# GpSimd's four stores of a turned tile ahead of the next tile load, in a hybrid mLSTM / RWKV-7 / attention / PEER layer

## The reference, cut to what matters

```python
# per block of 128 tokens, 8 heads, 16 experts of 16384 a head
top, pos = lax.top_k(cand, PK_TOPK)          # cand: sums of two sets of 16 scores
eidx = jnp.take_along_axis(cidx, pos, axis=-1)
gate = jax.nn.softmax(top, axis=-1)
act = jax.nn.gelu(jnp.einsum('thkd,td->thk', u_tab[eidx], xb), approximate=False)
return jnp.einsum('thk,thkd->td', gate * act, v_tab[eidx])
```

## Time and profile before

| | |
|---|---|
| time, median of 3 runs | 2667.21 us (2660.73 to 2667.88) |
| the profiled execution | 2662.08 us, of which the span from first to last instruction is 2660.3 us |
| TensorE busy, matmuls | 2383.6 us, 90% of the span |
| VectorE busy | 1722.8 us, 65% |
| GpSimd busy | 693.2 us, 26% |
| mean granted TensorE clock | 0.939 of full speed |
| tile loads by GpSimd (L532) | 120, of which 106 at depth 2 |
| stores of turned tiles (L537) | 512 |

### The profile page before, as it was taken

How to read it: one execution, slowest core, us unless ns; L and a number is a source line. 1 busy time by engine, 2 the same in 40 slices (tenths; PEclk the granted TensorE clock), 3 DMA queues, 4 the chain that set the end, 5 groups by cost and what they waited for, 6 DMA issues and landing times.

```text
span 2660.3 us, 41336 instructions
## 1 busy us (share of the span) xinstructions
PE 2383.6 (90%) x16321; PEld 2195.8 (83%) x16321; DVE 1722.8 (65%) x3186; ACT 914.0 (34%) x1569; POOL 693.2 (26%) x1003
## 2 busy tenths in 40 slices
PE   7976796887668989989899987999999999999997
PEld 5954675875546978888799987999999999999996
DVE  3545376434642444448979987887786478878876
ACT  2222243210111111112234355777784333333332
POOL 3300000011430555425521200333333032332330
PEclk9987898996886999999999989999999999999999
DMA  4520320013752899757775746999999799999993
GB/s 145 185 57 11 113 56 17 20 43 104 242 182 99 281 289 302 242 171 252 231 239 192 240 154 187 319 336 317 323 323 360 266 326 348 343 348 343 350 346 116
DMA packets 323185, 586.48 MB, mean 220 GB/s; under 512 B 26704, under 2 KB 217184, under 8 KB 321456
## 3 DMA queue, kind: packets, MB, share of 16 engines
q1 hardware_dynamic: 222960, 274.07, 31.5%
q0 software_dynamic: 81600, 282.49, 30.9%
q10 hardware_dynamic: 18432, 27.27, 2.8%
HBM read 455.09 MB, written 128.64 MB: 219 GB/s over the span
## 4 chain that ended last, share of the span: by engine, by line
PE 44%; DVE 13%; DMA 10%; ACT 3%; POOL 2%; issue 2%; ACTq 0%; DVEq 0%; POOLq 0%
PE PS L1075 43%; DMA u_rows<-arena 3%; DVE LO L2146 2%; DMA RAW<-in_uT 2%; DMA u_rows<-CBLK 2%; DMA GU<-u_rows,EIDX 2%; DVE OH L2279 2%; POOL u_rows L537 2%; DVE GU L2288 2%; ACT OH L1017 1%; ACT HI L979 1%; DVE arena L2243 1%; DVE arena L1677 1%; DVE arena L2234 1%; DVE arena L1638 1%
## 5 line engine op out<-in xcount | busy, mean ns | idle before, releaser
L2146 DVE TENSOR_TENSOR LO<-RAW,HI 128x1024 fp32r<-128x1024 f32 x256 | 313.1, 1225 | 234.5 <-ACT HI L979 233.8
L979 ACT ACTIVATE HI<-RAW 128x1024 fp32r<-128x1024 f32 x256 | 270.3, 1056 | 551.5 <-PE PS L1075 503.7
L1075 PE MATMUL PS<-HT,W 128*128 128x272 f32 (+1 forms) x1536 | 374.9, 405 | 18.5 <-DVE HT L1689 12.5
L1075 PE MATMUL PS<-XH,HI 128*128 128x416 f32 x1024 | 369.8, 361 | 10.1 <-issue 8.4
L1075 PEld LDWEIGHTS PS<-HT,W 128*128 128x128 f32 (+1 forms) x1536 | 292.2, 192 | 94.8 <-issue 18.4
L1075 PE MATMUL PS<-XH,LO 128*128 128x416 f32 x1024 | 364.1, 356 | 0.0
L1075 PE MATMUL PS<-WH,HI 128*128 128x416 f32 x1024 | 360.4, 352 | 1.4 <-DVE WL L2161 1.4
L1075 PE MATMUL PS<-XL,HI 128*128 128x416 f32 x1024 | 361.6, 353 | 0.0
L1075 PE MATMUL PS<-WL,HI 128*128 128x416 f32 x1024 | 359.6, 351 | 0.0
L1075 PE MATMUL PS<-WH,LO 128*128 128x416 f32 x1024 | 357.4, 349 | 0.0
L1075 PE MATMUL PS<-arena 64*64 64x64 f32 (+10 forms) x3864 | 275.0, 261 | 49.8 <-DVE arena L1638 23.6
(11 more groups left out here) (262 smaller groups left out, 3639.8 us busy)
## 6 DMA issues: line engine op xcount, KB each, us to landing
RAW<-in_uT SPq DMA_DIRECT2D x128, 512.0 KB, 5.3
RAW<-in_vT SPq DMA_DIRECT2D x128, 512.0 KB, 5.7
arena<-in_uT POOLq DMA_DIRECT2D x90, 512.0 KB, 5.3
W<-in_w_in SPq DMA_DIRECT2D x58, 512.0 KB, 5.4
u_rows<-arena POOLq DMA_DIRECT2D x216, 128.0 KB, 4.0
table_a<-AX ACTq DMA_DIRECT2D x128, 208.0 KB, 4.6
gate_table<-GST SPq DMA_DIRECT2D x13, 2048.0 KB, 13.7
AIN<-table_a SPq DMA_DIRECT2D x128, 208.0 KB, 6.7
```

What stands on the lines that cost most here:

```text
L979: nc.scalar.activation(HI[:, s % NRING], RAW[:, s % NRING], ACT.Copy).then_inc(S("hi"), 1)
L1075: return nc.tensor.matmul(out, lhsT, rhs, start=first, stop=last)
L2146: dve.tensor_tensor(LO_[:, s % NRING], RAW[:, s % NRING], HI[:, s % NRING].bitcast(F32), ALU.subtract).then_inc(S("lo"), 1)
```

## The change

In the stages of depth 2, GpSimd issues the four stores of tile k first and the load of tile i = k + 2 behind them. In the stages of depth 1 the order stays: load, then stores. The load is moved into a function of its own, and nothing else differs: the same DMAs, buffers, semaphores and waits.

```diff
+            def load_tile(phase, i):
+
+                first, n, depth = TILES[phase]
+                if i < first + n and phase != "E":
+                    pool.dma_start(tile_in[phase][(i - first) % depth],
+                                   a["uT"][:, tile_chunk(i)].rearrange("p k n -> p (k n)")).then_inc(S(f"tin{i % 2}"), 16)
+
             def turn_tiles(phase):

                 first, n, depth = TILES[phase]
                 for i in range(first, first + n + depth):
                     k = i - depth
                     if k >= first:
                         pool.wait_ge(S("tr"), k + 1)
-                    if i < first + n and phase != "E":
-                        pool.dma_start(tile_in[phase][(i - first) % depth],
-                                       a["uT"][:, tile_chunk(i)].rearrange("p k n -> p (k n)")).then_inc(S(f"tin{i % 2}"), 16)
+                    if depth == 1:
+                        load_tile(phase, i)
                     if k >= first:
                         rows, turned = u_rows[tile_chunk(k)].rearrange("(b c) q x -> q c b x", b=4), tile_out[phase][(k - first) % depth]
                         for q in range(4):
                             pool.dma_start(rows[q], turned[32 * q:32 * q + 32].rearrange("c (b x) -> c b x", b=4)
                                            ).then_inc(S(f"tout{k % 2}"), 16)
+                    if depth == 2:
+                        load_tile(phase, i)
                 for i in range(2):
                     pool.wait_ge(S(f"tout{i}"), 64 * ((first + n + 1 - i) // 2))
```

## The result

The changed kernel takes 2679.06 us, median of 7 runs (2672.27 to 2681.64), against 2666.69 us for the kernel before (7 runs, 2660.73 to 2668.43). The ratio is 1.0056, with a 95% interval of 1.004 to 1.0072: slower. The two medians lie 12.4 us apart, the ratio stands for 15 us, and the interval holds both. The profiled execution took 2679.06 us, its span is 2677.3 us, 17.0 us over the span before. 2676 us was forecast.

A forecast was written before the change was run, and what follows sets the result against it. The loop of turning tiles was taken to bound stage G, and DVE's list the end of Q. G 6.6, A 0.9 and Q 2.1 us sum to 9.6 us on the 2667.2 us median, so 2676 us, range 2658 to 2690.

The forecast's parts named there:

- The bound: Stage G: the loop of turning tiles, 9.50 us, sets the pace, though TensorE is busy 191.3 of 206 us.
- The swap of the last DMA: Depth-2 loops: last issue stays at the same moment but becomes a 512 KB load instead of a 128 KB store.
- The signs: G: 30 or more of 44 waits on loads, landing 5.5 to 6.5 us, loop 9.8; first PEER product 10 us later.
- The three terms of the sum: Added time at 0.3 us a tile: G 22 loops, 6.6 us; A 3 loops, 0.9; Q 7 transposes, 2.1.
- X: Time in a tile's loop from GpSimd's first issue to the last landing, some 7.88 us in G; forecast to grow 0.3.
- X in a quiet queue: Last landing with little other traffic: 5.4 us before, 6.3 after, so growth of 0.9 us (0.84 unrounded).
- the estimate of one third of the way: Growth per loop taken one third from full queue (0) to quiet queue (0.9 us): 0.3 us.
- Q: End of stage Q: DVE's list sets TensorE's 8.40 us gap, so seven transposes each 0.3 us later cost 2.1 us.
- Order doesn't matter: Rival for G, A, Q: queue full enough, loop grows 0 to 0.2 us, 2667 to 2673 us; chance 0.32.
- The stores were the slow part, and the load lands soon enough: Rival: load lands within 5.1 us, loop falls up to 0.56 us, 2650 or 2658 us; chance of faster 0.13.
- The load is in the open everywhere: Rival: full 0.84 us per loop, G 18.5, A 2.5, Q 5.9, 27 us, so 2694 us; chance 0.13 (above 0.5).

The follow-up runs named there:

- g3_stores_first: Kernel before plus a third input buffer in stage G, with the four stores issued ahead of the load there: 2641.96 us, ratio 0.9928.
- g3_load_first: Kernel before plus a third input buffer in stage G, load still issued first: 2660.62 us, ratio 0.9994.
- the quarter loads: Two kernels, G's loads cut to 256 of 1024 columns against the kernel before: 2645.3 us load first, 2640.1 us stores first, one run each.
- the two experiments on the parts: Kernel before with stores ahead of the load in G alone: 2673.24 us, 1.0039; in N, A and Q alone: 2671.85 us, 1.003.
- gq3_stores_first: Kernel before plus a third input buffer and stores ahead of the load in both G and Q: 2642.63 us, ratio 0.9924.
- the run second: Kernel before with the load issued behind one store and ahead of three in every stage of depth 2: 2680.4 us, one run.

## Why the prediction was right

*The bound.* That the loop of transposes sets G, and not TensorE with its 93%, is shown by g3_stores_first against g3_load_first: the same DMAs and buffers in another order, a shorter loop, and 19 us less.

*The swap of the last DMA.* The step "the last DMA of a loop is issued at the same moment as before; it is now a load of 512 KB in place of a store of 128 KB" is shown by the chain after, by the 41 waits that moved from stores to loads, and by the quarter loads, which take the difference in size away and the loss with it.

*The signs.* Named beforehand were waits on the load, 30 or more (41), its landing at 5.5 to 6.5 us (6.0), a loop of 9.8 us (9.87), and TensorE's wait at about 20 us (22.7). The first PEER product was to start 10 us later; it started 17.0 us later.

*The size.* The three terms of the sum were all too small:

| place | forecast | the profiled pair | means of all profiles of either order |
|---|---|---|---|
| one loop in G | +0.3 us | +0.37 us | +0.30 us by one parity, +0.38 by all 44 transposes |
| G | +6.6 us | +10.1 | +8.1 |
| A | +0.9 us | +3.2 | +3.4 |
| Q | +2.1 us | +3.8 | +5.0 |
| all | +9.6 us | +17.0 | +12.4 by the medians |

The last column's parts sum to more than the 12.4 us, and so do the two experiments on the parts, 18.4 us; both sums still lie inside the interval of the whole change, which is 10.7 to 19.2 us.

The mis-sized term is X in a quiet queue. I took the load's quiet landing, 4.1 us, from a load that went first, and used it for a load that goes last. Behind four stores it is 5.0 us in the mean of four, so the quiet end of the range for X was not 6.3 - 5.4 = 0.9 us but 2.18 + 5.0 - 5.4 = 1.7. The fit of the Trainium skill (DMA: Bandwidth & Descriptors, section Anatomy of one DMA) knows no place in the queue; with it the difference of load and store would be 0.9 us by estimate wherever they stand, and these rows don't agree. A and Q, where the queue is less full than in G, lie nearer to that end, and there I was furthest off: the last landing of a tile came 0.7 us later in A and 0.9 in Q, and 0.4 in G (means of all profiles of either order, against a forecast of 0.3 in each). In G the estimate of one third of the way held because two errors (an end that was too low, a weight that was too high) offset each other. That was luck, and so is a part of how near the predicted 2676 us came.

*Q.* That TensorE's gap at the end of Q belongs to DVE's list is borne out by two things: the gap grew by 3.84 us while Q's transposes spread by 3.8, and in each of the twelve profiles the first PEER product starts 0.1 us after the end of DVE's first low part, with gaps of 3.8 to 12.2 us. Shortening the list pays only until ScalarE's high part is what DVE waits for, as gq3_stores_first shows.

*The rivals.* "Order doesn't matter" and its full queue: refuted, the engines moved 322 GB/s in g3_stores_first and the ratio of the change excludes 1. "The stores were the slow part, and the load lands soon enough": its first half was true, they land 0.7 us sooner by the median when they go first; its second half failed, for the load needed to land within 5.1 us of its issue and took 6.0. With the load made to matter no longer, that first half alone gave the 0.7%. "The load is in the open everywhere", 27 us, was about twice too much, and its error lay in G, 18.5 us for 8 to 10; in A (2.5 us) and Q (5.9) it was nearer than my forecast.

## What to carry to other kernels

Before DMAs are reordered because an engine waits for one of them, look for what else the same engine waits for next: if the one put off is needed at the same point, the loop ends with whichever is issued last, and the largest transfer costs most in that place. Price a DMA in its new place in the queue, not from where it stood. To make the order pay, take the other transfer out of the loop, here with a third input buffer: in G 0.7% faster with both, nothing with the buffer alone, 0.4% slower with the order alone.

## What the hardware showed that I had not expected

A load of 512 KB on GpSimd's queue landed 4.0 to 4.4 us after its issue when it went first (14 loads in seven profiles), and 4.8 to 5.4 us after it when one, two, three or four stores of 128 KB stood ahead (10 loads in five profiles), in a stretch with little else to move. The cost was not smaller for one store than for four. It isn't the bytes ahead either: at the start of G two loads are issued 0.53 us apart, and the second, with 512 KB ahead of it, landed 4.6 to 4.8 us after its issue in the ten profiles with full loads, sooner than the two loads behind one store (5.3 us). In the run second the traffic held at 20 to 60 GB/s for most of a microsecond before the load's flow began. No run here shows whether it is the issue, the descriptors or the memory.

The slowest order, the load third, gave 2685 us by the median of four runs while its profiled execution took 2676 and has a shorter loop than the changed kernel. The profiled one was the fastest of the four, so its trace doesn't tell what the others did.
